# Layer 1's conditioning vectors: products on VectorE, sums over the partitions on TensorE

## The reference, cut to what matters

```python
def modulation(cond, w_mod, b_mod):
    m = jax.nn.silu(cond) @ w_mod + b_mod          # (1024) @ (1024, 6144), for c and for c_ctx
    return jnp.split(m, 6, axis=-1)

def modulate(x, g, shift, scale):
    return rms_norm(x, g) * (1.0 + scale[:, None, :]) + shift[:, None, :]

def swiglu(h, w_in, w_out):
    a, b = jnp.split(h @ w_in, 2, axis=-1)
    return (jax.nn.silu(a) * b) @ w_out

for l in range(DEPTH):                             # DEPTH = 2
    sh1, sc1, gt1, sh2, sc2, gt2 = modulation(c, w_mod[l], b_mod[l])
    ...
    xl = xl + gt1[:, None, :] * mix_l
    xl = xl + gt2[:, None, :] * swiglu(modulate(xl, g_ffn[l], sh2, sc2), w_ffn_in[l], w_ffn_out[l])
```

## Time and profile before

| | us |
|---|---|
| median of 3 runs | 2443.41 (2441.47 to 2445.3) |
| the profiled execution, its own time | 2444.06 |
| its span in the profile | 2442.2 |
| busy: PE / PEld / DVE / ACT / POOL | 2125.6 / 1721.2 / 1009.6 / 731.9 / 622.6 |

### The profile page before, as it was taken

How to read it: one execution, slowest core, us unless ns; L and a number is a source line. 1 busy time by engine, 2 the same in 40 slices (tenths; PEclk the granted TensorE clock), 3 DMA queues, 4 the chain that set the end, 5 groups by cost and what they waited for, 6 DMA issues and landing times.

```text
span 2442.2 us, 29454 instructions
## 1 busy us (share of the span) xinstructions
PE 2125.6 (87%) x11680; PEld 1721.2 (70%) x11680; DVE 1009.6 (41%) x1794; ACT 731.9 (30%) x1190; POOL 622.6 (25%) x820
## 2 busy tenths in 40 slices
PE   1877899978888799999999967798988877999998
PEld 1666788856667588788878864677865555888886
DVE  1565634367775421112102155564357885212111
ACT  2243232335553311111111132332334543222221
POOL 0111120221001232323233321112131102555554
PEclk9988999989989799999999988998899998999999
DMA  6200232110001133223223211011010001222222
GB/s 261 80 18 18 88 124 93 44 35 9 18 9 35 60 119 115 69 95 130 86 78 120 88 46 35 18 37 44 30 57 18 18 9 35 95 95 95 95 95 95
DMA packets 76238, 165.54 MB, mean 68 GB/s; under 512 B 5192, under 2 KB 46664, under 8 KB 75088
## 3 DMA queue, kind: packets, MB, share of 16 engines
q1 hardware_dynamic: 75728, 163.28, 20.3%
q10 hardware_dynamic: 384, 0.47, 0.1%
HBM read 161.63 MB, written 2.10 MB: 67 GB/s over the span
## 4 chain that ended last, share of the span: by engine, by line
PE 72%; DVE 14%; ACT 6%; issue 5%; DMA 1%; SPq 1%; POOL 1%; DVEq 0%; ACTq 0%; POOLq 0%
PE psum L958 20%; PE psum L959 19%; PE psum L960 19%; PE psum L1009 2%; DMA marope<-c_rope 1%; DVE naptlo L1774 1%; PE psum L1019 1%; PE psum L1460 1%; DVE n_t L1651 1%; PE psum L1116 1%; DVE n_t L1679 1%; DVE hlo L1671 1%; DVE xres L1695 1%; PE psum L1231 1%; PE psum L1245 1%
## 5 line engine op out<-in xcount | busy, mean ns | idle before, releaser
L471 POOL TENSOR_TENSOR wlo<-raw,whi 128x256 fp32r<-128x256 f32 x816 | 622.4, 795 | 1806.8 <-ACT whi L497 1806.8
L958 PE MATMUL psum<-hhi,whi 128*128 128x512 f32 (+1 forms) x1640 | 592.2, 361 | 36.7 <-DVE hlo L1671 14.3
L959 PE MATMUL psum<-hlo,whi 128*128 128x512 f32 (+1 forms) x1640 | 584.1, 356 | 0.0
L960 PE MATMUL psum<-hhi,wlo 128*128 128x512 f32 (+1 forms) x1640 | 583.4, 356 | 0.0
L497 ACT ACTIVATE whi<-raw 128x1024 fp32r<-128x1024 f32 x204 | 215.2, 1058 | 935.0 <-PE psum L960 934.7
L958 PEld LDWEIGHTS psum<-hhi,whi 128*128 128x128 f32 x1640 | 316.2, 193 | 94.0 <-issue 23.2
L960 PEld LDWEIGHTS psum<-hhi,wlo 128*128 128x128 f32 x1640 | 315.9, 193 | 43.2
L959 PEld LDWEIGHTS psum<-hlo,whi 128*128 128x128 f32 x1640 | 316.7, 193 | 40.3
L2171 DVE TENSOR_TENSOR ffuf<-ffsa,psum 128x768 f32<-128x768 f32 (+1 forms) x44 | 36.1, 821 | 534.4 <-ACT ffsa L910 534.4
L958 PE MATMUL psum<-uhi,whi 128*128 128x512 f32 (+1 forms) x528 | 190.8, 361 | 8.3 <-POOL wlo L471 7.5
L960 PE MATMUL psum<-uhi,wlo 128*128 128x512 f32 (+1 forms) x528 | 189.6, 359 | 0.0
(11 more groups left out here) (297 smaller groups left out, 3318.5 us busy)
## 6 DMA issues: line engine op xcount, KB each, us to landing
raw<-w_stream SPq DMA_DIRECT2D x204, 512.0 KB, 3.5
wm<-w_mod SPq DMA_DIRECT2D x80, 512.0 KB, 4.9
wm<-w_mod SPq DMA_DIRECT2D x8, 1024.0 KB, 17.9
xres<-x_t SPq DMA_DIRECT2D x8, 384.0 KB, 6.1
out<-xres SPq DMA_DIRECT2D x8, 256.0 KB, 2.9
consts<-c_f SPq DMA_DIRECT2D x1, 353.0 KB, 7.6
narpb<-rpb ACTq DMA_DIRECT2D x2, 120.0 KB
mlmask<-c_gate ACTq DMA_DIRECT2D x2, 108.0 KB
```

The costliest lines, as they stand in the source:

```text
L471: ins = nc.gpsimd.tensor_tensor(wlo[:, q % 2, c:c + UW // 4], raw[:, q % RAW, c:c + UW // 4], whi[:, q % 2, c:c + UW // 4], ALU.subtract)
L958: mm(dst, ah, bh, start=first, stop=False)
L959: mm(dst, ah, bl, start=False, stop=False)
L960: return mm(dst, al, bh, start=False, stop=last)
```

## The change

TensorE's `ring_chunk` and `mod_turn` and ScalarE's `mod_row_of` are gone for layer 1. DVE forms the products instead: `mod_product(n)` multiplies the eight 128-row tiles of a chunk with the silu of the condition, a scalar per partition, and accumulates them in `macc` (128 x 256 for c and for c_ctx, two buffers), 16 instructions per chunk with a wait on `mod_sums` between each two and a drain with an increment of `mod_c` behind each half. PE's `mod_sum(n)` adds `macc` up over the partitions: 4 matmuls with 128 x 128 of `macc` as weights and one column of ones moving. The products of chunk MODN(j) stand behind the `ulo` of slot j, those of the extra chunk behind the residual of m = 1; the sums stand one slot later, and at m = 3. `load_mod` is unchanged, so a ring buffer now comes free when DVE has used it. Layer 0's conditioning keeps the old way.

```diff
--- before.py
+++ after.py
@@ -167,7 +167,7 @@
             return d
 
         def ff_scope(a):
-            return dict(uhi=a("uhi", [P, 8, TOK], fp32r), ulo=a("ulo", [P, 8, TOK], fp32r),
+            return dict(macc=a("ffmacc", [P, 2, 2, 256]), uhi=a("uhi", [P, 8, TOK], fp32r), ulo=a("ulo", [P, 8, TOK], fp32r),
                         sa=a("ffsa", [P, 2, TOK]), uf=a("ffuf", [P, 2, TOK]))
 
         RNG, NRM, NA, ML, MA, FF = (scope(f) for f in (ring_scope, norm_scope, na_scope, ml_scope, ma_scope, ff_scope))
@@ -187,6 +187,7 @@
         pe_phase, act_phase, dve_phase = sem("pe_phase"), sem("act_phase"), sem("dve_phase")
         act_chain, dve_chain = sem("act_chain"), sem("dve_chain")
         mod_c, mod_row, mod_tr, mod_add = (sem(x) for x in ("mod_halves", "mod_rows", "mod_turned", "mod_added"))
+        mod_sums = sem("mod_sums")
         sq_done, sq_used, st_done = sem("sq_done"), sem("sq_used"), sem("st_done")
         r_done, t_done, h_hi, h_lo = sem("r_done"), sem("t_done"), sem("h_hi"), sem("h_lo")
         s_ps, s_nmx, s_exp, s_rs = (sem(x) for x in ("scores", "negmax", "exps", "inv_rowsum"))
@@ -908,12 +909,8 @@
                         act.wait_ge(w_used, u + 2)
                         act.wait_ge(ff_free, l * HG + j + 1)
                         A(FF["sa"][:, par, q0:], ff_psum(par, 0, full), ACT.Silu).then_inc(ff_sa, 1)
-                        if l == 0:
-                            mod_row_of(1, MODN(j), bank(6)[:, 0:256])
                         his(min(u + 6, b + 2 * n + 2))
                     his(u0(l, FF_OUT[g]) + 4)
-                    if l == 0 and g < len(FF_GROUPS) - 1:
-                        mod_row_of(1, MODN(j0 + n) - 1, bank(6)[:, 0:256])
                     his(u0(l, FF_OUT[g]) + KT + (2 if g < len(FF_GROUPS) - 1 else 0))
                     j0 += n
 
@@ -1029,6 +1026,17 @@
                     pe.wait_ge(ring_in[h % RING], 16 * (h // RING + 1))
                     return RNG["wm"][:, h % RING, :, :]
                 mod_chunk(l, n, bank(6) if dst is None else dst, src)
+
+            def mod_sum(n):
+
+                e = MODC + n
+                pe.wait_ge(mod_c, 2 * (e + 1))
+                for u in range(2):
+                    for c in range(2):
+                        at = 4 * n + 2 * u + c
+                        ins = mm(bank(7)[:, at:at + 1], FF["macc"][:, n % 2, c, P * u:P * u + P], ones[:, 0:1],
+                                 start=True, stop=True)
+                ins.then_inc(mod_tr, 1)
 
             def mod_head():
 
@@ -1556,10 +1564,8 @@
                         for ab in range(2):
                             ff_in_unit(b + 2 * (j - j0) + ab, j % 2, ab, full,
                                        tiles=16 * l + KT if j == ab == 0 else None)
-                        if l == 0:
-                            ring_chunk(1, MODN(j))
-                            if MODN(j):
-                                mod_turn(1, MODN(j) - 1, bank(7))
+                        if l == 0 and MODN(j):
+                            mod_sum(MODN(j) - 1)
                     pe.wait_ge(ff_free, l * HG + j0 + n + 1)
                     for m in range(KT):
                         unit(bo + m)
@@ -1567,11 +1573,7 @@
                         feature_unit(bo + m, m % 2, ranges(full), tiles_of(FF["uhi"]), tiles_of(FF["ulo"]), nk=n,
                                      last=l * HG + j0 + n + 2 if m == 0 else None)
                         if l == 0 and m == 3:
-                            if g < len(FF_GROUPS) - 1:
-                                ring_chunk(1, MODN(j0 + n) - 1)
-                                mod_turn(1, MODN(j0 + n) - 2, bank(7))
-                            else:
-                                mod_turn(1, MODC - 1, bank(7))
+                            mod_sum(MODN(j0 + n) - 2 if g < len(FF_GROUPS) - 1 else MODC - 1)
                     j0 += n
 
             for l in range(DEPTH):
@@ -2159,6 +2161,27 @@
                             probs_lo(h, i)
 
 
+            def mod_product(n):
+
+                e = MODC + n
+                if n >= 2:
+                    dve.wait_ge(mod_tr, e - 1)
+                for half in range(2):
+                    h = 2 * (e - MOD_HEAD) + half
+                    dve.wait_ge(ring_in[h % RING], 16 * (h // RING + 1))
+                    for j in range(4):
+                        if half or j:
+                            dve.wait_ge(mod_sums, 8 * n + 4 * half + j)
+                        for c in range(2):
+                            acc, k = FF["macc"][:, n % 2, c, :], 4 * half + j
+                            w, x = RNG["wm"][:, h % RING, j, :], csil[:, k, c:c + 1]
+                            if k:
+                                ins = V.scalar_tensor_tensor(acc, w, x, acc, ALU.mult, ALU.add)
+                            else:
+                                ins = V.tensor_scalar(acc, w, x, None, ALU.mult)
+                        ins.then_inc(mod_sums, 1)
+                    V.drain().then_inc(mod_c, 1)
+
             def ff_dve(l, full):
                 q0 = 0 if full else CTX_LEN
                 j0 = 0
@@ -2173,6 +2196,8 @@
                         V.tensor_copy(hi_, uf).then_inc(ff_uhi, 1)
                         dve.wait_ge(ff_uhi, l * HG + j + 1)
                         V.tensor_tensor(lo_, uf, hi_, ALU.subtract).then_inc(ff_free, 1)
+                        if l == 0:
+                            mod_product(MODN(j))
                     for m in range(KT):
                         dve.wait_ge(w_used, bo + m + 1)
                         for r0, r1 in ranges(full):
@@ -2180,6 +2205,8 @@
                                                          mods[:, l, 40 + m, cls(r0):cls(r0) + 1],
                                                          xres[:, m, r0:r1], ALU.mult, ALU.add)
                         ins.then_inc(x_free, 1)
+                        if l == 0 and m == 1 and g < len(FF_GROUPS) - 1:
+                            mod_product(MODN(j0 + n) - 1)
                     j0 += n
                 if l == 0:
                     mod_take(1, 0, MODC, bank(7))
```

## The result

| | before | after |
|---|---|---|
| median, us | 2444.36 (2441.47 to 2449.01, 4 runs) | 2415.6 (2410.95 to 2417.24, 4 runs) |
| ratio | | 0.9885, 95% interval 0.9863 to 0.9906 |
| span of the profiled execution, us | 2442.2 | 2414.4 |

The change is faster by 1.15%, some 28.8 us by the medians and 27.8 us by the spans. The forecast was 2420 in a range of 2412 to 2432, a gain of 23.8.

The account below looks back on a forecast made before the run. PE was taken as the bound, with every matmul in layer 0's FFN paid for. The terms -24.0 + 11.3 - 11.6 + 0.5 = -23.8 us, from the profiled 2444.06, gave 2420.3, so 2420, range 2412 to 2432.

Parts of the forecast that it names:

- The chunk matmuls go: Layer 0's FFN on PE: 24 chunks of 1.00 us each leave the path, -24.0 us.
- The turn becomes the sum: PE between slots: 4 records become 8, +0.47 us, 24 times, +11.3 us.
- exposed weight loads: Rival at PE's sums: eight weight loads that don't overlap, 1.52 us a sum, 2434 us; 8%.
- The stall goes: Groups 1 and 2 across m = 3: unit 4's rounding no longer queued behind ACT's copy, -11.6 us.
- The products cost nothing: DVE in the slots: products of about 7.2 us, covered by 5.3 us before PE wants them, cost 0.
- The ring: Weight ring: buffers come free about 8 us later, but weights are wanted one and a half slots later, 0.
- The second part: Extra products between residuals, and group 3's m = 0 residual at +13.7 against +14.6: just covered, 0, up to 2.
- Given back in front of the last `ulo`: Group 3's second part, first unit: PE arrives 0.53 us earlier and waits as much longer, +0.5 us.
- POOL starving in the second part: Rival in groups 1 and 2: DVE holds POOL up, the old stall returns, gain 12.2, 2432 us; 8%.
- The late product: Rival in the slots: products of 14 us, PE waits 1.6 us behind 22 slots, 2455 us, slower; 4%.
- The clock stayed at 1.00: Answers a rival at the sums: the clock falls there, some 2.4 us each, 2470 us; 1%.

Follow-up runs that it names:

- e10: Changed kernel with the eight old 32-column matmuls put back ahead of 21 sums, results unused; slots of 18.79 us against 17.56.
- e9: Kernel before with one of the turn's two matmuls left out for layer 1's chunks; slots of 18.11 us, 0.24 less.
- e7: Changed kernel with only one of the four matmuls of each sum; 2395.68 us, ratio 0.9802.
- e1: Kernel before with groups 1 and 2's extra-chunk modrow copy issued behind the roundings of units 4 and 5; 2428.93 us, ratio 0.9952.
- e2: Changed kernel with ScalarE made to wait, behind unit 3's rounding in groups 1 and 2, for TensorE's sum; 2423.37 us, ratio 0.9927.
- e4: Changed kernel with four more unused VectorE instructions per chunk (20 for 16); slots stayed at 17.56 us, the FFN stretch grew by 3.1 us.
- e5: Changed kernel with sixteen more unused VectorE instructions per chunk (32 for 16); 2502.94 us, ratio 1.0245.
- e6: Changed kernel with the 14 accumulating instructions of a chunk reading their third operand from an unused PSUM bank; FFN stretch 1.33 us shorter.
- e8: Changed kernel with the second half of the very last chunk's products moved behind group 3's residual of m = 0; 2408.7 us, ratio 0.9857.

## Why the prediction was right, and where it was off

The forecast was right in kind and 4.6 us short on the stretch (23.8 for 28.45). By its own steps:

1. *The chunk matmuls go* (-24.0). This was the term that was mis-sized most. I took 1.00 us, from the first record of the chunk to the first of the turn, and left out what lies around it. e10 measured 1.23 us a chunk, so -29.5 for 24. The hint was in the rows: 0.32 us from the last big matmul to the chunk where the pace was 0.23, and the slot itself, 18.34 us, which was 1.7 longer than two units of 8.3 while my pieces made 1.47. I had put 0.17 us of gaps into the stall's arithmetic and as a chance of -3.7 us into the range, but not into the sum.
2. *The turn becomes the sum* (+11.3). The two are 0.90 against 0.46 or 0.47 us, +0.43, or 10.4 in all. The pace of the turn was right (e9: 0.12 a record), that of the sum a little quicker (e7: 0.105). The rival of exposed weight loads, 1.52 us a sum, is out.
3. *The stall goes* (-11.6). Right, by two experiments from two sides, 11.76 taken away in e1 and 12.61 put back in e2.
4. *The products cost nothing* in the slots: right, and e4 and e5 show the edge on both sides: a quarter more is still free there, twice as much is 57 us slower than the kernel before. A product without the collision took 7.13 us (e6, 7.2 foreseen), but 9.0 to 9.1 in the slots: it met 3.5 us of POOL's work where "under 2 us" was written, and VectorE's busy time rose by 203 us for a foreseen 180. I had allowed for about half of that in the slots, where the cover took it, and for nothing in term 6.
5. *The ring*: no wait for a weight transfer or a ring buffer shows in the changed kernel's FFN. Right.
6. *The second part* (0, up to 2). The place in group 3 was named, "just covered", and it wasn't: the residual of m = 0 ended at 1362.3, +15.6 where +13.7 was foreseen and +14.6 allowed, and TensorE waited 1.1 us for it; e6 and e8, without that wait, had a stretch 1.3 us shorter. The 1.8 us that the Trainium skill's rule gave for this place was nearer than my 0. In groups 1 and 2 the cover held.
7. *Given back in front of the last `ulo`* (+0.5): 0.87 us of wait stands there, and it takes back the 0.8 us by which TensorE's work behind the last slot had become shorter (from the last `ffuf` to the residual of m = 3 it is 25.14 us in the kernel before and in e8 alike).

The measured terms make, in the order of terms 1, 2, 3, 6 and 7, -29.5 + 10.4 - 11.8 + 1.3 + 0.8 = -28.8, beside the stretch's -28.45. Of the rivals, POOL starving in the second part didn't come about: its pieces took 3.31 us beside the extra product of group 1, and no PE wait followed. The late product is real, but only from a longer product than this one, and then it costs more than its lateness, since the clock falls behind it (e4, e5); its rival had counted the lateness alone. The clock stayed at 1.00 through the slots with their sums.

## What to carry to other kernels

When work leaves the engine that bounds, a good part of the gain may lie in what its results held up: here 11.8 of 28 us came from ScalarE no longer queueing a copy ahead of the next weight rounding, and a one-line reorder of the kernel before gets that without the rest. Price a group of odd-shaped matmuls by the difference between the whole beat and a beat without it, not by the distance between its own records. And before putting filler work on an idle engine, look at each place where something short and due stands behind it: split the filler there. Price a wait of the bounding engine with what the clock costs behind it: in e5 that was some 38 us on top of 55 of waiting.

## What the runs showed of the hardware

- The eight 32-column matmuls cost 1.23 us among 128-column ones where their 16 records span 1.00 (e10).
- Float32 matmuls with 128 x 128 weights and a single moving column cost 0.105 us a record, two records an instruction, though each weight load is shown as 0.19 us long (e7 and the changed kernel).
- A `scalar_tensor_tensor` with two SBUF tensors and GpSimd's `tensor_tensor` slow each other, 3.60 to 5.48 us for eight and 2.83 to 3.38 for four; with the second tensor in PSUM neither is slowed (e6).
- Pauses of TensorE in this FFN of up to 1.50 us left the granted clock at 1.00 (e7 has the longest such one), and so did the sums' 0.8 us of little work. Every pause of 2.23 us or more was followed by a stretch at 0.50, the 1.2 GHz level (e5 2.23 to 6.37, e4 2.62, the kernel before 3.76, e9 3.98, e2 3.99 us).
